# Seven block products for eight in the up projection of an MLP, with the down projection cut into pieces that follow it

## The chip, the cores and the metric

The kernel runs on one core of a Trainium2 chip. The metric is the device time of one execution in microseconds (us). The program is one launch with five instruction streams: TensorE (PE in the profile) multiplies matrices, VectorE (DVE), ScalarE (ACT) and GpSimd (POOL) do elementwise work, SyncE (SP) issues the loads of weights. Streams meet only at semaphores that the code counts by hand. Each stream runs in program order, so an instruction that waits holds up everything behind it on its engine.

## The reference, cut to what matters

Two blocks work on a 1024 x 1024 activation in float32: first an attention layer and a convolution layer, then a recurrent mixer and an MLP. Only the MLP at the end is changed:

```python
h = rms_norm_2(x, norm_mlp[l])
x = x + jnp.square(jax.nn.relu(h @ w_up[l])) @ w_down[l]   # w_up 1024 x 4096, w_down 4096 x 1024
return rms_norm_2(x, norm_final)
```

## The kernel before, in words

**Layout.** Everything stays in SBUF with channels on the 128 partitions and 1024 tokens along the free axis. `X[:, k, :]` is channel tile k (0 to 7) of the residual stream. A matmul takes a weight tile of 128 x 128 and 512 tokens and accumulates into one PSUM bank of 512 float32. PSUM has eight banks; `acc(0)` is banks 0 and 1, `acc(1)` banks 2 and 3, `bank(b)` one of them.

**Split operands.** TensorE works in the rounded type fp32r, so each operand is kept as a high part and the remainder: `Whi`, `Wlo` for weights, `Hh`, `Hl` for the normalised input, `Bh`, `Bl` for other activations. Each product is a triple (`triple`, lines 1500 to 1502): high x high, high x low, low x high.

**A unit.** A unit is one weight slab of 1024 rows x 128 columns: eight tiles, two halves of the tokens, three matmuls, so 48 matmuls (`whole`, `half`). SyncE loads the slab into `Wraw[:, slot]`, ScalarE copies it to `Whi` once TensorE is done with the slab two units before (line 487), GpSimd subtracts to get `Wlo` (line 404), and TensorE waits for that (`claim`). There are two slots, so a slab is prepared while the one before it is multiplied.

**The MLP.** 4 rounds (`for c in range(4)`): eight units of `w_up`, then eight of `w_down` over the 1024 hidden channels just made. ScalarE applies relu (`ut`), VectorE squares it (`sq2`, line 1472), ScalarE copies the square to `Bh`, VectorE subtracts to get `Bl` (line 1475). A down unit is added to `X` by VectorE (line 1479). The last eight down units go by token halves (`by_halves`, called from line 2057, with `projection(3, ...)` on the other engines): units 0 and 1 whole, then six half-token pieces of the first half and six of the second, 24 matmuls each. While these run, the final norm is built up: for each piece n VectorE adds PSUM to `X` (`residual`, line 1260), ScalarE squares (line 506), VectorE adds the square to `sacc` (`add_square`, line 924). After the first token half TensorE sums `sacc` over the channels with a matrix of ones (`square_sum`, line 1544), ScalarE takes the root (line 510), VectorE the reciprocal (line 929) and scales two tiles per piece (line 935). The second token half then ends in the same way, and the results are stored.

**Entry.** The MLP is entered through `opening`: two up units, multiplied half by half as VectorE finishes the normalised input (line 942).

Of the kernel before, what the change touches and what calls it, by code (L numbers as in the profile page):

```python
# [47 lines left out]
def columns_of(params):  # L48
    at, out = 0, {}
    for name, rows in params:  # L50
# [10 lines left out]
          ("rg", 32), ("hg", 40), ("ho", 14), ("mlp", 70)]  # L61
# [49 lines left out]
def build(nc, I, out_dram):  # L111
# [63 lines left out]
    tn = at("tn", T + 12 * KB, [2, 512])  # L175
    Bh = at("Bh", y0, [KT, N], F32R)
# [82 lines left out]
    ut = at("ut", T, [2, N])  # L259
    sq2 = at("sq2", T + 8 * KB, [2, N])  # L260
# [10 lines left out]
    raw_free = sem("raw_free")  # L271
# [10 lines left out]
    DOWN = BASE["mlp"] + 56  # L282
# [17 lines left out]
    w_down = nW["w_down_2"][0].rearrange("(c k p) m -> p c k m", p=P, k=KT)  # L300
# [5 lines left out]
    def sp_program(sp):  # L306
# [23 lines left out]
        for h in range(2):  # L330
            c = slice(h * 512, h * 512 + 512)
            for j in range(4):
                sp.dma_start(X[:, 2 * j:2 * j + 2, c], xk[:, 2 * j:2 * j + 2, c]).then_inc(sem(f"x_loaded{h}{j}"), 16)
# [51 lines left out]
        for c in range(4):  # L385
            for j in range(8):
                unit_at(BASE["mlp"] + 16 * c + j, c * 1024 + j * P, w_up)
            if c < 3:
                for j in range(8):
                    unit_at(BASE["mlp"] + 16 * c + 8 + j, j * P, w_down[:, c, :, :])  # L390
        projection_weights(DOWN, w_down[:, 3, :, :])
# [81 lines left out]

    gate = lambda l: 24 * l + 16
# [3 lines left out]
    def act_program(act):  # L478
# [16 lines left out]
        def projection(i, base, shift):  # L495

            def square(n):
                evacuated(act, 0, 2, base + n)
# [31 lines left out]
        act.wait_ge(sem("eps_set"), 1)  # L530
        act.activation(cs[:, :, 0], P1[:, COL1["c"]:COL1["c"] + 8], ACT.Silu).then_inc(sem("cs_ready"), 1)
        act.activation(cs[:, :, 1], P1[:, COL1["c_ctx"]:COL1["c_ctx"] + 8], ACT.Silu).then_inc(sem("cs_ready"), 1)
        act.wait_ge(sem("lb_shifted"), 1)
        act.activation(small[:, 0:8], small[:, 0:8], ACT.Exp).then_inc(sem("lb_exp"), 1)
        act.wait_ge(sem("lam_abs"), 1)
        act.activation(small[:, 32:40], small[:, 24:32], ACT.Exp, scale=-1.0).then_inc(sem("lam_exp"), 1)
        act.wait_ge(sem("lamsum"), 1)
        act.activation(small[:, 8:10], bank(0, 2), ACT.Exp).then_inc(sem("lamexp"), 1)
        for n in range(2 * KT):
            h, k = n // KT, n % KT  # L540
            act.wait_ge(sem(f"x_loaded{h}{k // 2}"), 16)
# [344 lines left out]
        for c in range(4):  # L886
            for k in range(8):
                u = BASE["mlp"] + 16 * c + k
                if c and k == 0:
                    split_next(0, 2, u)  # L890
                got(act, 0, 2, u)
                split_next(0, 2, u + 1)
                act.wait_ge(sem("ut_free"), c * 8 + (k + 1))
                act.activation(ut[:, k % 2, :], acc(k % 2), ACT.Relu).then_inc(acc_free[k % 2], 1)  # L894
                act.wait_ge(sem("usq_ready"), c * 8 + (k + 1))
                act.activation(Bh[:, k, :], sq2[:, k % 2, :], COPY).then_inc(sem("uh_ready"), 1)
            for k in range(1, 8 if c < 3 else 0):
                split_next(0, 2, BASE["mlp"] + 16 * c + 8 + k)
        projection(3, DOWN, None)


    def dve_program(dve):
        stt, tt, ts = dve.scalar_tensor_tensor, dve.tensor_tensor, dve.tensor_scalar

        def projection(i, base, add_to, gain, shift):

            H, L = ((Bh, Bl), (Bh, Bl), (Hh, Hl), (None, None))[i]

            def residual(n):
                u = base + n  # L910
# [21 lines left out]
            def scaled(h, k):  # L932
# [43 lines left out]
        dve.memset(EPSC, EPS).then_inc(sem("eps_set"), 1)  # L976
# [3 lines left out]
        tt(small[:, 0:8], lbl, lbl, ALU.subtract).then_inc(sem("lb_shifted"), 1)  # L980
# [4 lines left out]
        dve.drain().then_inc(sem("lamprod"), 1)  # L985
# [3 lines left out]
        dve.drain().then_inc(sem("lam_abs"), 1)  # L989
# [57 lines left out]
        dve.wait_ge(sem("lam_exp"), 1)  # L1047
# [24 lines left out]
        dve.wait_ge(sem("lb_exp"), 1)  # L1072
# [12 lines left out]
        dve.wait_ge(sem("lamexp"), 1)  # L1085
# [381 lines left out]
        for c in range(4):  # L1467
            for k in range(8):
                u = BASE["mlp"] + 16 * c + k
                dve.drain()  # L1470
                evacuated(dve, 0, 2, u)
                tt(sq2[:, k % 2, :], ut[:, k % 2, :], ut[:, k % 2, :], ALU.mult).then_inc(sem("usq_ready"), 1)  # L1472
                dve.drain().then_inc(sem("ut_free"), 1)
                dve.wait_ge(sem("uh_ready"), c * 8 + (k + 1))
                tt(Bl[:, k, :], sq2[:, k % 2, :], Bh[:, k, :].bitcast(F32), ALU.subtract).then_inc(sem("ul_ready"), 1)
            for k in range(8 if c < 3 else 0):
                u = BASE["mlp"] + 16 * c + 8 + k
                got(dve, 0, 2, u)
                tt(X[:, k, :], X[:, k, :], acc(k % 2), ALU.add).then_inc(acc_free[k % 2], 1)  # L1479
            dve.drain()  # L1480
        projection(3, DOWN, plain, lambda k: P2[:, COL2["norm_final_2"] + k:COL2["norm_final_2"] + k + 1], None)


    def pe_program(pe):
# [56 lines left out]
        def square_sum(i, h):  # L1541

            pe.wait_ge(sem("sq_added"), 12 * i + 5 * h + 7)
            ins = mm(bank(4 + h), ones, sacc[:, h, :], start=True, stop=(h == 0))
            if h:
                pe.wait_ge(sem("sq_ready"), 14 * i + 14)
                ins = mm(bank(5), ones, sqs[:, 1, :], start=False, stop=True)
# [37 lines left out]
        pe.wait_ge(sem("lamprod"), 1)  # L1585
# [35 lines left out]
        def first_products(k, h):  # L1621
# [3 lines left out]
            for u in range(2):  # L1625
                if k == 0 and h == 0:
                    pe.wait_ge(lo_ready, u + 3)
                    pe.wait_ge(sem("lamexp"), 1)
# [6 lines left out]
        pe.wait_ge(sem("cs_ready"), 2)  # L1635
# [414 lines left out]
        for c in range(4):  # L2050
            b = BASE["mlp"] + 16 * c
            for j in range(0 if c else 2, 8):
                whole(b + j, (Hh, Hl))
            pair(b + 8, (Bh, Bl), lambda h, k: pe.wait_ge(sem("ul_ready"), c * 8 + k + 1))
            for j in range(2, 8 if c < 3 else 0):
                whole(b + 8 + j, (Bh, Bl))
# [57 lines left out]
```

## Time and profile before

| what | value |
|---|---|
| median of 3 runs | 2892.82 us (2890.85 to 2893.32) |
| profiled execution, its own time | 2892.7 us |
| its span in the trace | 2890.9 us |
| TensorE busy over the span | 2820.3 us, 98% |
| VectorE, ScalarE, GpSimd busy | 1432.4, 913.5, 627.4 us |
| mean granted TensorE clock | 0.997 of full |

The span runs from the first to the last recorded instruction; the execution's own time is 1.8 us longer. Times in the rows are microseconds from the span's start. The MLP lies from about 2177 to 2891.

### The profile page before, as it was taken

The page shows a single profiled execution, that of the slowest core. Times are in us where ns is not written, and L with a number is a line of the kernel's source. Part 1 is how long each engine was busy: PE and PEld are TensorE (multiplying, and loading weights), DVE is VectorE, ACT ScalarE, POOL GpSimd, SP SyncE. Part 2 cuts the span into 40 slices and gives each one's busy share as a digit, 9 for nine tenths or more (in the row PEclk, how much of TensorE's full clock was granted, in tenths as well). Part 3 has the DMA queues.
Part 4 walks back from the last instruction along what each step waited for, and adds up shares of the span by engine and source line. Part 5 has one row for each costly group of instructions (what it writes and reads, how often), then busy time and mean ns, then how long its engine had stood idle before and what let it go on. Part 6 is the DMA issues. An engine that isn't in the chain of part 4 may idle for free.

```text
span 2890.9 us, 34606 instructions
## 1 busy us (share of the span) xinstructions
PE 2820.3 (98%) x14290; PEld 2338.5 (81%) x14290; DVE 1432.4 (50%) x1518; ACT 913.5 (32%) x1087; POOL 627.4 (22%) x319
## 2 busy tenths in 40 slices
PE   7999999999999999999999999999999999999997
PEld 4878777887788888788888888888777888888886
DVE  6478128877422226545555665656765213131236
ACT  4332217763211113444442222222333112121122
POOL 0111115104222224222221111111142222212222
PEclk9999999999999999999999999999999999999999
DMA  7211440023111112111111111111031111111113
GB/s 225 73 29 39 150 147 1 1 74 95 51 45 51 47 49 84 55 44 44 51 55 37 37 30 37 37 37 37 23 85 54 47 49 44 52 51 51 44 54 114
DMA packets 276884, 168.52 MB, mean 58 GB/s; under 512 B 5632, under 2 KB 270208, under 8 KB 276352
## 3 DMA queue, kind: packets, MB, share of 16 engines
q1 hardware_dynamic: 275296, 162.88, 19.2%
q10 hardware_dynamic: 1440, 3.51, 0.3%
q8 instruction: 113, 1.85, 0.3%
q14 instruction: 35, 0.29, 0.0%
HBM read 162.17 MB, written 4.19 MB: 58 GB/s over the span
## 4 chain that ended last, share of the span: by engine, by line
PE 60%; issue 27%; POOL 5%; DVE 4%; ACT 2%; DVEq 1%; SPq 0%; DMA 0%; POOLq 0%; ACTq 0%
PE PS L1500 16%; PE PS L1502 16%; PE PS L1501 16%; POOL Wlo L404 5%; PE PS L1948 3%; ACT exp L689 1%; DVE acol L1177 1%; PE PS L1676 1%; PE PS L1597 1%; PE PS L1953 1%; PE PS L1813 1%; PE PS L1982 1%; PE PS L1936 0%; PE PS L1685 0%; PE PS L1984 0%
## 5 line engine op out<-in xcount | busy, mean ns | idle before, releaser
L404 POOL TENSOR_TENSOR Wlo<-Wraw,Whi 128x1024 fp32r<-128x1024 f32 x237 | 564.5, 2382 | 1992.2 <-ACT Whi L487 1992.2
L1500 PE MATMUL PS<-Bh,Whi 128*128 128x512 f32 x2176 | 858.6, 395 | 3.5 <-POOL Wlo L404 1.3
L1502 PE MATMUL PS<-Bh,Wlo 128*128 128x512 f32 x2176 | 848.1, 390 | 0.0
L1501 PE MATMUL PS<-Bl,Whi 128*128 128x512 f32 x2176 | 847.5, 389 | 0.0
L487 ACT ACTIVATE Whi<-Wraw 128x1024 fp32r<-128x1024 f32 x237 | 247.2, 1043 | 767.4 <-PE PS L1502 765.1
L1500 PEld LDWEIGHTS PS<-Bh,Whi 128*128 128x128 f32 x2176 | 409.1, 188 | 93.2 <-DVE Bl L942 4.9
L1502 PEld LDWEIGHTS PS<-Bh,Wlo 128*128 128x128 f32 x2176 | 408.7, 188 | 86.3
L1501 PEld LDWEIGHTS PS<-Bl,Whi 128*128 128x128 f32 x2176 | 409.1, 188 | 82.9 <-issue 1.0
L1500 PE MATMUL PS<-Hh,Whi 128*128 128x512 f32 x1120 | 443.9, 396 | 4.9 <-issue 1.7
L1502 PE MATMUL PS<-Hh,Wlo 128*128 128x512 f32 x1120 | 436.2, 389 | 0.0
L1501 PE MATMUL PS<-Hl,Whi 128*128 128x512 f32 x1056 | 411.2, 389 | 0.0
L1500 PEld LDWEIGHTS PS<-Hh,Whi 128*128 128x128 f32 x1120 | 210.3, 188 | 57.7 <-issue 12.4
L1502 PEld LDWEIGHTS PS<-Hh,Wlo 128*128 128x128 f32 x1120 | 210.2, 188 | 44.4
L1501 PEld LDWEIGHTS PS<-Hl,Whi 128*128 128x128 f32 x1056 | 198.3, 188 | 41.6 <-issue 1.7
L1472 DVE TENSOR_TENSOR sq<-ut 128x1024 f32<-128x1024 f32 x32 | 83.7, 2616 | 197.0 <-ACT ut L894 197.0
L1479 DVE TENSOR_TENSOR X<-X,PS 128x1024 f32<-128x1024 f32 x24 | 29.3, 1221 | 214.3 <-PE PS L1502 214.3
L1336 DVE COPY_PREDICATED hP<-mk,PS 127x512 f32<-127x512 int32 (+6 forms) x56 | 50.1, 894 | 105.4 <-PE PS L1948 105.2
L1948 PEld LDWEIGHTS PS<-hZ 128*127 128x127 f32 (+6 forms) x896 | 93.1, 176 | 8.2 <-issue 3.1
L1948 PE MATMUL PS<-hZ 128*127 128x64 f32 (+6 forms) x896 | 93.7, 257 | 2.3 <-DVE hZ L1350 2.1
L689 ACT ACTIVATE exp<-PS,acol 128x1280 f32<-128x1280 f32 x60 | 79.6, 1327 | 43.9 <-DVE acol L1179 43.6
L924 DVE TENSOR_TENSOR sacc<-sacc,sqs 128x512 f32<-128x512 f32 x44 | 75.5, 1716 | 25.6 <-ACT sqs L506 25.6
L1840 PE MATMUL PS<-vT,probT 128*128 128x128 f32 x640 | 76.8, 275 | 0.4 <-ACT osq L703 0.4
(329 smaller groups left out, 3083.9 us busy)
## 6 DMA issues: line engine op xcount, KB each, us to landing
Wraw<-in_w_in SPq DMA_DIRECT2D x64, 512.0 KB, 4.0
Wraw<-in_w_down SPq DMA_DIRECT2D x38, 512.0 KB, 3.7
adaV<-in_ada_w SPq DMA_DIRECT2D x16, 1024.0 KB, 5.2
Wraw<-in_odd_w_in SPq DMA_DIRECT2D x32, 512.0 KB, 4.1
Wraw<-in_w_up SPq DMA_DIRECT2D x32, 512.0 KB, 4.1
Wraw<-in_even_w_in SPq DMA_DIRECT2D x24, 512.0 KB, 3.8
adaW<-in_ada_w SPq DMA_DIRECT2D x8, 1024.0 KB, 11.3
Wraw<-in_even_w_out SPq DMA_DIRECT2D x14, 512.0 KB, 3.8
```

The source lines that it names most:

```text
L404: pool.tensor_tensor(Wlo[:, slot, 0:tiles, :], Wraw[:, slot, 0:tiles, :], Whi[:, slot, 0:tiles, :].bitcast(F32), ALU.subtract).then_inc(lo ...
L487: act.activation(Whi[:, slot, 0:tiles, :], Wraw[:, slot, 0:tiles, :], COPY).then_inc(hi_ready, 1)
L689: act.activation(weights_of(b, m)[:, :], PS[:, (S0, S1)[m]:(S0, S1)[m] + NK], ACT.Exp, bias=acol[:, b % 3, 5 + m:6 + m], accum_out=acol[:, ...
L924: tt(sacc[:, h, :], sacc[:, h, :], sqs[:, n % 2, :], ALU.add).then_inc(sem("sq_added"), 1)
L1336: dve.copy_predicated(hP[0:r, :].rearrange("p (c b two l) -> p c b two l", c=8, two=2, l=L)[:, :, :, 1, :], mk[lev][0:r, :].rearrange("p ( ...
L1472: tt(sq2[:, k % 2, :], ut[:, k % 2, :], ut[:, k % 2, :], ALU.mult).then_inc(sem("usq_ready"), 1)
L1479: tt(X[:, k, :], X[:, k, :], acc(k % 2), ALU.add).then_inc(acc_free[k % 2], 1)
L1500: mm(out, Whi[:, u % 2, k, :], hi[:, k, c], start=(k == 0), stop=False)
L1501: mm(out, Whi[:, u % 2, k, :], lo[:, k, c], start=False, stop=False)
L1502: return mm(out, Wlo[:, u % 2, k, :], hi[:, k, c], start=False, stop=(k == KT - 1))
L1840: ins = mm(rows_in(b), probT[:, b % 2, t, :], vT[:, t, h * P:(h + 1) * P], start=(t == 0), stop=(t == 9))
L1948: ins = mm(bank(4 + lev % 2, 64, c * 64)[0:P - L].rearrange("p (b l) -> p b l", l=L), z[:, 0:P - L], right, start=True, stop=True)
```

## The change

The first four up units stay as they were, and a down piece over their 512 hidden channels follows at once. The other 28 up units are taken two at a time, 14 pairs. A pair is a 256-column slab of `w_up` times 1024 tokens. It is cut into 2 x 2 blocks (rows of weights 0 to 511 and 512 to 1023 against two output tiles; channels against token halves), and its four output quadrants C11, C12, C22, C21 are made from seven block products (Strassen in Winograd's form) in place of eight. A block product is 4 tiles x 3 matmuls = 12 matmuls of 512 tokens.

- **Token sums.** Four sums of blocks of the normalised input are made once, before the pairs (`difference`, and the plain `tt` beside it), split into high (`token_high`) and low (`token_low`, for the last block VectorE inside pair 0).
- **Weight sums.** Four sums of blocks of weights per pair are made by GpSimd (`first_sums`, `second_sum`, `third_sum`), and each of the seven blocks is split as before, by halves of a slot (`block_high` on ScalarE, `part_low` on GpSimd). A block's high part is written once the product four before it is done.
- **Products.** They share banks: products 3, 4 and 5 are added onto what a bank holds, after ScalarE has copied the earlier value out (`product_out`). VectorE adds the copy and the bank (`quadrant`), squares with relu in one instruction (`squared`), ScalarE makes the high part (`u_high`), VectorE the low (`quadrant_low`).
- **Down pieces.** After each odd pair but the last (2 pairs = 4 hidden tiles) come four down units of 48 matmuls. The first of them uses the four older quadrants first, and asks for the newest low parts in two steps.
- **End.** The last four hidden tiles are multiplied in 14 steps (`last_products`): two of 24 matmuls, then twelve of 12.
- **Memory.** Two more raw slots and a sum buffer are placed in memory gained by `dynamic_dma_scratch_size=1024`; some semaphores are merged.

The diff, cut to its core:

```diff
-          ("rg", 32), ("hg", 40), ("ho", 14), ("mlp", 70)]
+          ("rg", 32), ("hg", 40), ("ho", 14), ("mlp", 4)]
...
+    BUF_OF = {C11: 0, C12: 1, C22: 2, C21: 0}
+    COPIED = {0: (C11, 3), 2: (C22, 1), 3: (C12, 3), 5: (C21, 3)}
+    FINAL = {C11: (1, 0), C12: (4, 1), C22: (5, 3), C21: (6, 2)}
...
 # SyncE
+        def pair_loads(g):
+            n = pair_load(g)
+            for u in range(2):
+                sp.wait_ge(sem("up_lo"), down_event(g // 2 - 1, 2 * (g % 2) + u) + 1)
+                col = (FIRST + 2 * g + u) * P
+                raw_load(n + u, raw_of(n + u), w_up[:, :, col:col + P])
...
 # GpSimd
+        token_low(0)
+        down_low(-1, 0)
+        down_low(-1, 1)
+        token_low(1)
+        token_low(2)
+        down_low(-1, 2)
+        down_low(-1, 3)
+        for g in range(PAIRS):
+            first_sums(g)          # 2 sums, drain
+            second_sum(g)          # low part of block 0, 1 sum, drain
+            third_sum(g)           # low part of block 1, 1 sum, drain
+            other_lows(g)          # low parts of blocks 2 to 6, drain
+            if g % 2 and g < 12:
+                for d in range(4):
+                    down_low(g // 2, d)
...
 # ScalarE
+        def product_out(g, i):
+            q, b = COPIED[i]
+            act.wait_ge(sem("product"), 7 * g + i + 1)
+            if q == C21:
+                act.wait_ge(sem("ul_ready"), 8 + 4 * g + 1)
+            else:
+                act.wait_ge(sem("ul_ready"), 4 + 4 * g + (4 if q == C11 or g == 0 else q + 1))
+            act.activation(cbuf[BUF_OF[q]][:, :], pair_bank(g, b), COPY).then_inc(sem("product_out"), 1)
...
+        first_relu(0)
+        first_u(0)
+        token_high(0)
+        first_relu(1)
+        first_u(1)
+        token_high(1)
+        token_high(2)
+        first_relu(2)
+        down_high(-1, 0)
...
+        for g in range(PAIRS):
+            for i in range(7):
+                p = 7 * g + i
+                if i == 0 and g % 2:
+                    u_high(g - 1, C21)
+                if i in COPIED:
+                    product_out(g, i)
+                if not ends or i < 3:
+                    block_high(p + 4)
+                elif c == RUNS - 1:
+                    last_high(i - 3)
+                elif i in (4, 6):
+                    down_high(c, i // 2 - 2)
+                if i in (2, 5, 6):
+                    u_high(g, {2: C11, 5: C12, 6: C22}[i])
+                if g == 0 and i == 1:
+                    act.wait_ge(sem("down_psum"), SMALL)
+                    token_high(3)
...
 # VectorE
+        for k in range(4):
+            first_half_again(k, k)             # one scalar_tensor_tensor each
+        for k in range(4):
+            first_half_again(12 + k, 4 + k)
+        dve.drain()
+        for k in range(4):
+            difference(k, 8 + k, k)
+        first_squares(0)                       # 2 squares, 2 low parts
+        for k in range(4):
+            tt(Tf[:, 8 + k, :], Tf[:, 4 + k, :], Tf[:, 8 + k, :], ALU.subtract)
+        first_squares(1)
+        for k in range(4):
+            difference(4 + k, 4 + k, k)
+        dve.drain()
+        for k in range(4):
+            difference(12 + k, 12 + k, 4 + k)
+        first_squares(2)
+        first_squares(3)
...
+        for g in range(PAIRS):
+            quadrant(g, C11)
+            quadrant_low(g, C11)
+            if g == 0:
+                ...                            # 4 low parts of the fourth token block
+            quadrant(g, C12)
+            quadrant(g, C22)
+            quadrant_low(g, C12)
+            quadrant(g, C21)
+            quadrant_low(g, C22)
+            quadrant_low(g, C21)
...
 # TensorE
+        PRODUCT_BANK = (3, 0, 1, 3, 1, 3, 2)
+        def product(g, i):
+            p = 7 * g + i
+            out = pair_bank(g, PRODUCT_BANK[i])
+            pe.wait_ge(sem("up_lo"), block_event(p) + 1)
+            if i in (3, 4, 5):
+                pe.wait_ge(sem("product_out"), 4 * g + {3: 1, 4: 2, 5: 3}[i])
+            if g == 0 and i in (2, 3, 5, 6):
+                pe.wait_ge(sem("t_lo"), {2: 4, 3: 8, 5: 12, 6: 16}[i])
+            for k in range(4):
+                hi, lo = token_block(i, k)
+                ins = three(out, ..., k, hi, lo, ...)       # 3 matmuls of 512 tokens
+            ins.then_inc(sem("product"), 1)
...
+        for n in range(2, 14):
+            h = 0 if n < 8 else 1
+            pe.wait_ge(sem("up_lo"), last_event(n) + 1)
+            pe.wait_ge(sem("last_free"), n - 1)
+            last_products(n, h, (0, 1), halves[0])
+            if n == 9:
+                square_sum(3, 0)
+            last_products(n, h, (2, 3), halves[0]).then_inc(sem("last_ready"), 1)
...
-    nc = bacc.Bacc("TRN2", target_bir_lowering=False, num_devices=1)
+    nc = bacc.Bacc("TRN2", target_bir_lowering=False, num_devices=1, dynamic_dma_scratch_size=1024)
```

Four things in words. `down_low(-1, 0)` stands behind `token_low(0)`, which waits for eight `difference` steps. The high part of the fourth up unit is made in `first_relu(1)`, behind `first_u(0)` and `token_high(0)`. `last_free` is raised by VectorE's `residual`; `square_sum(3, 0)` has moved from the middle of piece 8 to the middle of piece 9. `last_high(n + 4)` stands ahead of the square of piece n.

## Rows read from the trace of the kernel before

**Rows 1.** The page, busy time and share of the span of each engine.

```profile
PE 2820.3 (98%) x14290; PEld 2338.5 (81%) x14290; DVE 1432.4 (50%) x1518; ACT 913.5 (32%) x1087; POOL 627.4 (22%) x319
```

**Rows 2.** Windows inside the MLP: bounds, length, each engine's busy time (instructions), granted clock, DMA.

```profile
2400.00:2600.00 200.00, 200.00 (x884) 165.62 (x883) 49.29 (x29) 38.80 (x38) 43.07 (x18) 1.00 0.17 50
```

**Rows 3.** Groups of instructions by form, 2197.9 to 2875.2: count, busy us, mean ns, idle before.

```profile
L1500 PE MATMUL PS<-Bh,Whi 128*128 128x512 f32 x512 | 199.6, 390 | 0.0
```

**Rows 4.** Groups of instructions by form, GpSimd.

```profile
L404 POOL TENSOR_TENSOR Wlo<-Wraw,Whi 128x512 fp32r<-128x512 f32 x8 | 10.3, 1287 | 68.7 <-ACT Whi L487 68.7
```

**Rows 5.** Groups of instructions by form, ScalarE.

```profile
L510 ACT ACTIVATE Rn<-PS,Dv 128x512 f32<-128x512 f32 x8 | 5.5, 687 | 21.3 <-PE PS L1544 13.5 <-PE PS L1547 7.8
...
L487 ACT ACTIVATE Whi<-Wraw 128x512 fp32r<-128x512 f32 x8 | 5.0, 621 | 0.0
```

**Rows 6.** Timeline of the end: start, length, engine, line, operation, idle before.

```profile
2840.15 0.69 DVE L1260 TENSOR_TENSOR X<-X,PS 128x512 f32<-128x512 f32 x1 [1.29 <-PE PS L1502]
2841.82 2.45 DVE L924 TENSOR_TENSOR sacc<-sacc,sqs 128x512 f32<-128x512 f32 x1 [0.98 <-ACT sqs L506]
2846.21 3.35 DVE L929 RECIPROCAL Rn<-Rn 128x512 f32<-128x512 f32 x1 [1.94 <-ACT Rn L510]
2849.64 0.69 DVE L1260 TENSOR_TENSOR X<-X,PS 128x512 f32<-128x512 f32 x1
2851.03 1.35 DVE L924 TENSOR_TENSOR sacc<-sacc,sqs 128x512 f32<-128x512 f32 x1 [0.70 <-ACT sqs L506]
...
2857.74 0.68 DVE L924 TENSOR_TENSOR sacc<-sacc,sqs 128x512 f32<-128x512 f32 x1
...
2870.59 1.41 DVE L935 SCALAR_TENSOR_TENSOR X<-X,P,Rn 128x512 f32<-128x512 f32 x2
...
2875.43 0.69 DVE L1260 TENSOR_TENSOR X<-X,PS 128x512 f32<-128x512 f32 x1 [2.83 <-PE PS L1502]
```

**Rows 7.** The same timeline: TensorE, ScalarE and GpSimd around 2841 to 2846.

```profile
2844.33 1.13 PE L1544 MATMUL PS<-sacc,basic 128*128 128x512 f32 x2 [1.50 <-DVE sacc L924]
...
2845.49 0.69 ACT L510 ACTIVATE Rn<-PS,Dv 128x512 f32<-128x512 f32 x1 [3.70 <-PE PS L1544]
...
2841.35 2.38 POOL L404 TENSOR_TENSOR Wlo<-Wraw,Whi 128x1024 fp32r<-128x1024 f32 x1 [3.04 <-ACT Whi L487]
```

**Rows 8.** Timeline, VectorE and GpSimd together in the attention stage and before the MLP.

```profile
447.50 0.46 POOL L448 TENSOR_TENSOR ql<-qT,qh 128x128 fp32r<-128x128 f32 x1
...
447.51 1.79 DVE L1195 SCALAR_TENSOR_TENSOR exp<-exp,acol,exp 128x1280 f32<-128x1280 f32 x1
...
447.89 2.52 POOL L437 CAST kh<-kT 128x1280 fp32r<-128x1280 f32 x1
...
2157.16 0.69 DVE L1260 TENSOR_TENSOR X<-X,PS 128x512 f32<-128x512 f32 x1
...
2157.25 2.40 POOL L404 TENSOR_TENSOR Wlo<-Wraw,Whi 128x1024 fp32r<-128x1024 f32 x1 [3.03 <-ACT Whi L487]
```

**Rows 9.** Timeline of the MLP's entry: VectorE, ScalarE, GpSimd.

```profile
2191.55 1.63 DVE L942 SCALAR_TENSOR_TENSOR Hl<-tn,Dv,Hh 128x512 fp32r<-128x512 f32 x2
...
2194.32 1.06 ACT L487 ACTIVATE Whi<-Wraw 128x1024 fp32r<-128x1024 f32 x1 [1.92 <-PE PS L1502]
...
2195.46 2.39 POOL L404 TENSOR_TENSOR Wlo<-Wraw,Whi 128x1024 fp32r<-128x1024 f32 x1 [18.80 <-ACT Whi L487]
```

**Rows 10.** Windows shortly before the MLP, columns as in rows 2.

```profile
2072.00:2076.00 4.00, 1.24 (x6) 1.25 (x7) 3.92 (x6) 0.11 (x1) 0.00 (x0) 0.53 0.00 0
2076.00:2080.00 4.00, 4.00 (x14) 3.26 (x13) 3.82 (x5) 1.02 (x1) 0.00 (x0) 0.62 0.00 0
```

**Rows 11.** Timeline of TensorE in the second of these windows.

```profile
2078.23 0.63 PE L1501 MATMUL PS<-Bl,Whi 128*128 128x512 f32 x1
2078.66 0.58 PE L1502 MATMUL PS<-Bh,Wlo 128*128 128x512 f32 x1
```

**Rows 12.** The page, DMA issues: KB each, median us from issue to landing.

```profile
Wraw<-in_w_up SPq DMA_DIRECT2D x32, 512.0 KB, 4.1
```

More of the change, by code:

```diff
@@ new lines, in act_program @@
+        down_high(-1, 2)
+        down_high(-1, 3)
+        for j in range(4):
+            block_high(j)
+        for g in range(PAIRS):
+            c = g // 2
+            ends = g % 2
+            for i in range(7):
[15 more added lines that the diff above has]
+                    token_high(3)
+            if ends:
+                u_high(g, C21)
+                if c < RUNS - 1:
+                    down_high(c, 2)
+                    down_high(c, 3)
+                    for j in range(4):
+                        block_high(14 * (c + 1) + j)
@@ new lines, in u_low, with first_squares @@
+        def u_low(b, tiles, n):
+            dve.wait_ge(sem("uh_ready"), n)
+            tt(tiles[1], cbuf[b][:, :], tiles[0].bitcast(F32), ALU.subtract).then_inc(sem("ul_ready"), 1)
+        def first_squares(u):
+            for h in range(2):
+                n = 2 * u + h
+                dve.wait_ge(sem("relu_out"), n + 1)
+                squared(FIRST_BUF[n], n)
+            for h in range(2):
+                n = 2 * u + h
+                u_low(FIRST_BUF[n], first_u_tiles(u, h), n + 1)
@@ new lines, in quadrant, with quadrant_low @@
+        def quadrant(g, q):
+            i, b = FINAL[q]
+            dve.wait_ge(sem("product"), 7 * g + i + 1)
+            dve.wait_ge(sem("product_out"), 4 * g + {C11: 1, C22: 4, C12: 3, C21: 4}[q])
+            buf = cbuf[BUF_OF[q]]
+            tt(buf[:, :], pair_bank(g, b), buf[:, :], ALU.add).then_inc(sem("quadrant_out"), 1)
+            dve.drain()
+            squared(BUF_OF[q], 8 + 4 * g + q)
+        def quadrant_low(g, q):
+            t, h = tiles_of(g)[q]
+            u_low(BUF_OF[q], (u_tile(Uh, Hh, t, h), u_tile(Ul, Hl, t, h)), 8 + 4 * g + q + 1)
@@ L2049, in pe_program, with three @@
         opening(2, BASE["mlp"], (Hh, Hl))
[L2050 to L2056, printed above, removed]
-        by_halves(3, DOWN, (Bh, Bl))
+        def three(out, place, w, hi, lo, first, last, onto=False):
+            mm(out, place(Whi, w), hi, start=first, stop=False, skip_group_check=onto)
+            mm(out, place(Whi, w), lo, start=False, stop=False, skip_group_check=onto)
+            return mm(out, place(Wlo, w), hi, start=False, stop=last, skip_group_check=onto)
@@ new lines, in pe_program @@
+        PRODUCT_BANK = (3, 0, 1, 3, 1, 3, 2)
[7 more added lines that the diff above has]
+                pe.wait_ge(sem("t_lo"), {2: 4, 3: 8, 5: 12, 6: 16}[i])
+            for k in range(4):
+                hi, lo = token_block(i, k)
+                ins = three(out, lambda W, n: part_of(W, block_place(p))[:, n, :], k, hi, lo, k == 0 and i in (0, 1, 2, 6), k == 3, i in (3, 4, 5))
+            ins.then_inc(sem("product"), 1)
@@ new lines, in pe_program, with last_products @@
+        for d in range(4):
+            down_unit(-1, d)
+        for g in range(PAIRS):
+            pair_banks_free(g)
+            for i in range(7):
+                product(g, i)
+            if g % 2 and g < 12:
+                for d in range(4):
+                    down_unit(g // 2, d)
+        def last_products(n, h, ks, c):
+            for k in ks:
+                ins = three(last_acc(n)[:, c], lambda W, m: part_of(W, last_place(n))[:, m, :], k,
+                            u_tile(Uh, Hh, k, h), u_tile(Ul, Hl, k, h), k == 0, k == 3)
+            return ins
```

406 lines of the change are left out of this document (337 added, 69 removed).

## Prediction

> **What bounds the kernel now.** I read four views in this order. The page's first part first: TensorE is busy 98% of the span, no other engine over 50% [rows 1]. Then the windows of the MLP: 200.00 of 200 us busy, 884 matmuls, clock full [rows 2]. The reader is to see the pace there, 200/884 = 0.2262 us for a matmul of 512 tokens; TensorE is not waiting, it is fully fed. Then the groups by form: the matmuls of the down units have 0.0 us of idle ahead of them [rows 3]. From 2197.9 to 2875.2 TensorE runs 2976 such matmuls; less 1.1 us for the two of ones and 1.5 us of waiting [rows 7], that is 674.7/2976 = 0.2267 us, which I use. Last the timeline, for what the other engines cost when they meet. So removed matmuls are worth their full time, and added work elsewhere is free until it makes TensorE wait.
>
> **What is removed.** Up before: 32 units x 48 = 1536 matmuls. After: 4 x 48 + 14 pairs x 7 products x 12 = 192 + 1176 = 1368. Down before 1536, after 8 x 4 x 48 less the last round, 7 x 192 + 2 x 24 + 12 x 12 = 1344 + 192 = 1536, the same. Removed: 168 matmuls x 0.2267 = **38.1 us**. A product of 12 lasts 2.72 us, a pair 19.04 (21.76 before), a down unit 10.88.
>
> **What is added, and where it hides.** GpSimd, per pair: 4 sums and 7 low parts, 11 instructions over 512 columns. The nearest row is 1.287 us [rows 4]; 14.2 us, under 19.04. ScalarE: 7 high parts and 4 high parts of quadrants at 0.62, 4 copies out of PSUM, of which the nearest row has 0.69 [rows 5]: 9.6 us. VectorE: 4 additions from PSUM at 0.69 [rows 6], 4 squares at 0.7 (1.41 for two) and 4 low parts at 0.68 [rows 6]: 8.3 us. Each fits alone. Cover is what TensorE has queued: a block's low part is ready up to four products (10.9 us) ahead.
>
> **The shared path.** VectorE's addition of two SBUF tiles takes 0.68 us alone [rows 6], but the one that started at 2841.82 took 2.45: GpSimd's subtraction ran 2841.35 to 2843.73 [rows 6, 7], and VectorE ended 0.54 after it. One with an operand in PSUM is not held (0.69 at 2157.16, beside GpSimd's 2157.25 [rows 8]). They take turns: VectorE's 1.79 began at 447.51, GpSimd's next, issued at 447.89, ended 1.11 us after it [rows 8]. The Trainium skill (GPSIMD Engine Reference, Specifications) says the same of the SBUF interfaces, which GpSimd shares with VectorE instructions that have two SBUF inputs; this trace agrees, 2.45 against 0.68. By that rule 8 of VectorE's 12 instructions per pair and all 11 of GpSimd's exclude each other.
>
> Both kinds together take 11 x 1.287 + 8 x 0.54 = 18.5 us of 19.04 in a pair. But down units follow each second pair with four low parts in 43.5 us, so only a lag within two pairs counts. One held VectorE instruction costs up to 1.287 + 0.54 = 1.83. I followed the tightest loop, from the last product of an even pair (time 0) to the odd pair's product 3, wanted at 3 x 2.72 = 8.2: it needs the old C21's low part, then a 0.7 copy. With every instruction held, C22 is squared at -0.1, C12's low part is done at 1.75, C21 is added at 2.5, squared at 4.4, low parts of C22 and C21 at 6.2 and 8.0, the copy at 8.7: late by 0.5. GpSimd's lead runs out before that (its next block must wait for this very copy), so the last two are not held. I take 0, bound 7 x 0.5 = 3.5. GpSimd from product 2 of the even pair (1.3 after it): 8 instructions x 1.287 + 7 turns x 0.54 = 15.4 until the odd pair's third block is ready, wanted at 4 + 2 products = 16.3: 0 again.
>
> **Pair 0.** Here VectorE has four more low parts, of the token block for product 6, behind C11's. From product 2's end: C11's high part 2.3, its low part 4.1, four held at 1.83 = 11.4; product 6 is due at 8.2. Stall between 0 and 3.3, taken **3.0**, since GpSimd has seven instructions in a row there.
>
> **Entry.** VectorE's last low part ends at 2193.2 [rows 9]. Then 8 instructions at 0.67, interrupted by GpSimd's subtraction (2195.46, 2.39 long): 2201.0; 4 differences 2203.6. Only then the first squares, 2205.0. GpSimd's subtraction waits for the one in progress, so the third up unit starts 2198.3, **0.4** later than before. ScalarE does `first_u(0)` (2205.7), `token_high(0)` (2208.1) and only then the fourth unit's high part (1.06, 2209.1); GpSimd its low part (2.39), 2211.6. TensorE is through with the third at 2209.2: wait **2.4**. The down piece's first low part stands behind `token_low(0)`, which needs eight differences. VectorE: low parts 2206.3, 4 subtractions 2208.8, squares held by GpSimd 2213.0, low parts 2214.3, differences 2216.8. Then 4 x 1.287 against 4 differences x 0.54 in turns: 2224.1; `down_low(-1, 0)` 2226.5. The fourth unit ends at 2222.5: wait **3.9**. Both waits have no cover; bounds 1 for the two together (the same chain with no instruction held) and 9.
>
> **End.** Count from the end of piece 7. Before, GpSimd held `add_square(7)`, so TensorE waited 1.5 [rows 7]. Now `square_sum(3, 0)` stands in piece 9, at 4.1. From it to the next `residual` is 1.16 to the root (2844.33 to 2845.49), 0.72 to the reciprocal, 3.43 to `residual(8)` (2849.64) [rows 6, 7]: 9.4. Piece 10 waits for that residual (10.0) and was due at 6.6. After it VectorE sets the pace: `residual` to `add_square` 1.39 (2849.64 to 2851.03), that 0.7, then four times 0.65 + 1.41 + 0.7, about 2.75 with 0.05 between: 13.3, so `residual(13)` at 22.7, plus 0.6 where GpSimd's last low part holds it: 23.3. TensorE alone would have it at 6 x 2.72 + 1.13 = 17.5, so 5.8 is waiting. Before, it came at 2875.43 - 2840.12 = 35.3 [rows 6], against 33.8: 1.5. The same work of VectorE now meets pieces half as long: net **+4.3**. What follows (2875.43 to the end) is the same. Bounds: +3 to +7.
>
> **Loads.** A slab lands 4.1 us after issue [rows 12]; the tightest is wanted more than a pair later. The last steps' half slabs are issued four steps (10.9) ahead: 0. GpSimd's and ScalarE's longer straight-line code, merged semaphores, the smaller descriptor memory: nothing waits on them in the rows, 0.
>
> **Clock.** After some matmul-poor microseconds the granted clock fell to 0.53 and 0.62 of full [rows 10], and 512-token matmuls came 0.43 us apart [rows 11], six in all, the 1.2 GHz level: 6 x 0.20 = 1.2 us. A wait of 1.5 us did not do it [rows 7]. Waits of 3 to 4 us are new here. I take one fall, **1.2**; bounds 0 and four falls, 4.8. The Trainium skill (TensorE: Matmul & The Clock Gate, What's actually happening) calls the slow state the default that activity releases. By that rule each long wait would be followed by a slow stretch.
>
> **Sum.** -38.1 + 0.4 + 2.4 + 3.9 + 3.0 + 4.3 + 1.2 = -22.9. The profiled execution took 2892.7 (span 2890.9, 1.8 around it), 0.1 under the median, so both give the same: 2892.7 - 22.9 = 2869.8, I say **2869.5**, span 2867.7.
>
> **Rivals.**
> A, the waits hide: 1 us at the entry, none in pair 0, the end as above: -38.1 + 4.3 + 1 = 2860. For it: my worst cases hold every instruction. Against: the entry's order is written down.
> B, the shared path sets the pace of pairs: if an instruction's start doesn't overlap the other's turn, 11 x 1.287 + 8 x (0.69 + 0.05 handover) = 20.1 per pair. 14 x (20.1 - 19.04) = 15 more: 2884. For it: 18.5 of 19.04 was already tight. Against: the down units give the lag back.
> C, slower: C21's chain makes product 3 of every odd pair wait. It decides where W plus a clock fall reaches 22.9/7 = 3.3 us, W = 2.1, that is a chain of 10.3 us for my 8.7 at most. At 12 us, 7 x (3.8 + 1.2) = 35: 2905. For it: seven engine changes in a row, each with a handover that I priced at 0.1. Against: 1.6 us beyond the bound. The clock page's rule, with a fall behind each wait, works in this direction.
> D, the gain is not there: 12-matmul products with three waits run at 0.2267 + 0.0082 = 0.235, 2808 x 0.0082 = 23 us lost, no change. Against: 24-matmul pieces show no such loss at their seams.
>
> **Chances.** Forecast 0.62, A 0.16, B 0.13, C 0.05, D 0.04. A measurement of this kernel can't tell changes under 0.2% (5.8 us) from none. Faster 0.91 (forecast, A, B), same 0.04 (D), slower 0.05 (C). The range takes in A below and B above: **2857 to 2888**.
>
> **What would show it.** In the trace after: 168 fewer 512-token matmuls at 0.227; one wait of TensorE of about 2.4 before the fourth up unit and one of 3.9 before the first down unit; one in pair 0 before product 6; none in later pairs; about 3.4 before piece 10 of the end; VectorE's squares in the pairs longer than 0.7 wherever GpSimd runs. I would be wrong if GpSimd's sums cost much more than 1.287, if TensorE waits in every pair on a copy or a low part, or if falls of the clock follow the waits and last.

## The result, and the profile after

The changed kernel takes 2868.65 us (2868.06 to 2869.2), against 2893.07 for the kernel before beside it: ratio 0.9918, 95% interval 0.9903 to 0.9933. It is faster by 24.4 us, 0.84%. On a second chip the ratio was 0.9919 (0.9906 to 0.9933). The forecast was 2869.5, a gain of 23. The profiled execution's own time is 2868.1, its span 2866.3, 24.6 less than before.

The page, busy time of each engine:

```profile
PE 2787.2 (97%) x14122; PEld 2309.0 (81%) x14122; DVE 1549.4 (54%) x1698; ACT 955.1 (33%) x1241; POOL 785.3 (27%) x461
```

Against [rows 1] TensorE has 14290 - 14122 = 168 matmuls fewer, as counted. VectorE has 117 us more, ScalarE 42, GpSimd 158. The windows say whether that costs anything:

```profile
2400.00:2600.00 200.00, 200.00 (x884) 165.58 (x884) 78.96 (x72) 46.73 (x74) 93.37 (x61) 1.00 0.16 48
...
2300.00:2800.00 500.00, 500.00 (x2208) 414.01 (x2207) 212.76 (x198) 131.50 (x213) 245.79 (x161) 1.00 0.17 52
```

Through 500 us of pairs and down units TensorE doesn't stop once, at the same 884 matmuls in 200 us as in [rows 2]. VectorE and GpSimd do far more than before and are hidden. So the price must lie at the ends. The waits of TensorE from 2135 on (who waited for whom: us in total, times, longest):

```profile
PE PS L2434 <- DVE X L1575: 3.6, 1, 3.6
PE PS L2434 <- POOL Wlo L645: 3.0, 1, 3.0
PE PS L1882 <- POOL Wlo L530: 2.0, 2, 1.3
PE PS L2434 <- DVE Tl L1852: 1.8, 1, 1.8
```

In this order they are the end (piece 10 waits for `residual(8)`), the first down unit (`down_low(-1, 0)`), the third and fourth up unit (0.7 and 1.3), and pair 0's product 6. Before, TensorE waited 1.5 at the end, for the sum [rows 7], and 0.3 ahead of the third up unit:

```profile
PE PS L1500 <- POOL Wlo L404: 0.3, 1, 0.3
```

This view counts idle time only. Lost time is the distance of two starts less the pace of 0.227: 1.4 us for the fourth up unit, 3.2 for the first down unit, 2.0 for product 6. The timeline shows what followed the 3.0, and the wait at the end:

```profile
2224.36 0.50 PE L2434 MATMUL PS<-Uh,Whi 128*128 128x512 f32 x1 [3.00 <-POOL Wlo L645]
2224.70 0.57 PE L2435 MATMUL PS<-Ul,Whi 128*128 128x512 f32 x1
2225.07 0.63 PE L2436 MATMUL PS<-Uh,Wlo 128*128 128x512 f32 x1
2225.49 0.63 PE L2434 MATMUL PS<-Uh,Whi 128*128 128x512 f32 x1
...
2837.08 0.77 PE L2434 MATMUL PS<-Uh,Whi 128*128 128x512 f32 x1 [3.63 <-DVE X L1575]
```

From the third on, starts are 0.43 apart, as in [rows 11], up to 2228.0; added up over nine distances, 1.6 us more is lost. I call a matmul slow when the next one starts 0.4 us or more after it: there are seven here. The granted clock of that window is 0.59, and 0.50 after the wait of 3.6 at the end, where 12 matmuls are slow:

```profile
2224.00:2228.00 4.00, 3.63 (x9) 2.88 (x10) 3.90 (x6) 3.11 (x6) 0.31 (x1) 0.59 0.47 131
...
2837.00:2841.00 4.00, 3.92 (x9) 3.14 (x10) 3.28 (x5) 1.75 (x3) 1.28 (x1) 0.50 0.00 0
```

Now the engines that caused this. Timeline of the entry and of pair 0, VectorE, ScalarE, GpSimd:

```profile
2192.71 7.51 DVE L1785 SCALAR_TENSOR_TENSOR Tf<-X,P,Rn 128x512 f32<-128x512 f32 x8
...
2212.60 9.52 DVE L1788 TENSOR_TENSOR Tf<-Tf 128x512 f32<-128x512 f32 x8
...
2206.65 1.04 ACT L681 ACTIVATE Whi<-Wraw 128x1024 fp32r<-128x1024 f32 x1
...
2215.16 6.40 POOL L611 TENSOR_TENSOR Tl<-Tf,Th 128x512 fp32r<-128x512 f32 x4 [5.03 <-ACT Th L1092]
2221.53 2.78 POOL L645 TENSOR_TENSOR Wlo<-Wraw,Whi 128x1024 fp32r<-128x1024 f32 x1
...
2280.95 6.85 DVE L1852 TENSOR_TENSOR Tl<-Tf,Th 128x512 fp32r<-128x512 f32 x4
2287.72 0.68 DVE L1812 TENSOR_TENSOR cbuf<-PS,cbuf 128x512 f32<-128x512 f32 x1
2288.49 1.00 DVE L1791 SCALAR_TENSOR_TENSOR cbuf<-cbuf 128x512 f32<-128x512 f32 x1
...
2291.13 1.78 DVE L1795 TENSOR_TENSOR Ul<-cbuf,Uh 128x512 fp32r<-128x512 f32 x1
```

Eight differences, 5 us when alone, take 9.5 while GpSimd's four token parts take 6.4 for 5.1: both lose by taking turns. GpSimd reaches the down piece's low part (2.78 for 2.40) only at 2221.5. In pair 0 four instructions of 0.68 take 6.85, 1.71 each; I had used 1.83. The last three rows show the sign that I had named: the addition from PSUM keeps its 0.68, the square beside it takes 1.00 for 0.7, the low part 1.78 for 0.68.

The end, VectorE's timeline, to be read beside [rows 6]:

```profile
2827.16 0.69 DVE L1575 TENSOR_TENSOR X<-X,PS 128x512 f32<-128x512 f32 x1
...
2832.82 3.35 DVE L1242 RECIPROCAL Rn_end<-Rn_end 128x512 f32<-128x512 f32 x1 [3.05 <-ACT Rn_end L709]
2836.25 0.69 DVE L1575 TENSOR_TENSOR X<-X,PS 128x512 f32<-128x512 f32 x1
...
2842.58 0.69 DVE L1575 TENSOR_TENSOR X<-X,PS 128x512 f32<-128x512 f32 x1 [1.29 <-PE PS L2436]
...
2850.84 0.69 DVE L1575 TENSOR_TENSOR X<-X,PS 128x512 f32<-128x512 f32 x1
```

From the end of piece 7 (2827.1) to `residual(8)` is 9.1 us, to `residual(13)` 23.7. The 1.29 of idle time at 2842.58 is VectorE waiting for TensorE, slowed by its clock.

### The profile page after: what moved, and what is told of

The parts are those of the page before. It is cut to its first block, busy times and chain, and to the rows that moved or that the text cites. A ratio compares the mean times of both kernels' runs of the same rounds, so it can differ in the third digit from the quotient of the medians.

```text
span 2866.3 us, 34875 instructions
## 1 busy us (share of the span) xinstructions
PE 2787.2 (97%) x14122; PEld 2309.0 (81%) x14122; DVE 1549.4 (54%) x1698; ACT 955.1 (33%) x1241; POOL 785.3 (27%) x461
## 3 DMA queue, kind: packets, MB, share of 16 engines
q8 instruction: 112, 1.84, 0.3%
## 4 chain that ended last, share of the span: by engine, by line
PE 60%; issue 25%; DVE 5%; POOL 5%; ACT 3%; DVEq 1%; DMA 0%; SPq 0%; ACTq 0%; POOLq 0%
PE PS L1882 9%; PE PS L1884 9%; PE PS L1883 9%; PE PS L2434 7%; PE PS L2436 7%; PE PS L2435 7%; POOL Wlo L530 5%; PE PS L2331 3%; ACT exp L892 1%; DVE acol L1492 1%; PE PS L2059 1%; PE PS L2336 1%; PE PS L1980 1%; PE PS L2196 1%; PE PS L2365 1%
## 5 line engine op out<-in xcount | busy, mean ns | idle before, releaser
L530 POOL TENSOR_TENSOR Wlo<-Wraw,Whi 128x1024 fp32r<-128x1024 f32 (+1 forms) x171 | 406.8, 2379 | 1491.8 <-ACT Whi L681 1491.7
L1882 PE MATMUL PS<-Bh,Whi 128*128 128x512 f32 x1664 | 659.0, 396 | 3.6 <-POOL Wlo L530 1.3
L1884 PE MATMUL PS<-Bh,Wlo 128*128 128x512 f32 x1664 | 648.8, 390 | 0.0
L1883 PE MATMUL PS<-Bl,Whi 128*128 128x512 f32 x1664 | 648.1, 389 | 0.0
L1882 PEld LDWEIGHTS PS<-Bh,Whi 128*128 128x128 f32 x1664 | 312.9, 188 | 73.3 <-DVE Bl L1257 5.2
L1884 PEld LDWEIGHTS PS<-Bh,Wlo 128*128 128x128 f32 x1664 | 312.4, 188 | 66.3
L681 ACT ACTIVATE Whi<-Wraw 128x1024 fp32r<-128x1024 f32 (+1 forms) x171 | 177.2, 1036 | 329.6 <-PE PS L1884 327.2
L604 POOL TENSOR_TENSOR Wlo<-Wraw,Whi 128x512 fp32r<-128x512 f32 x84 | 113.7, 1361 | 118.7 <-ACT Whi L1135 114.4
L645 POOL TENSOR_TENSOR Wlo<-Wraw,Whi 128x1024 fp32r<-128x1024 f32 x28 | 69.2, 2472 | 150.3 <-ACT Whi L1147 150.3
L2434 PE MATMUL PS<-Uh,Whi 128*128 128x512 f32 x256 | 101.1, 395 | 6.7 <-DVE X L1575 3.6
```

Of the source, the lines that this page charges most:

```text
L530: pool.tensor_tensor(Wlo[:, slot, 0:tiles, :], Wraw[:, slot, 0:tiles, :], Whi[:, slot, 0:tiles, :].bitcast(F32), ALU.subtract).then_inc(lo ...
L604: pool.tensor_tensor(part_of(Wlo, block_place(p)), raw, part_of(Whi, block_place(p)).bitcast(F32), sub).then_inc(sem("up_lo"), 1)
L645: pool.tensor_tensor(slot_of(Wlo, down_place(c, d)), raw_of(down_load(c, d)), slot_of(Whi, down_place(c, d)).bitcast(F32), sub).then_inc(s ...
L681: act.activation(Whi[:, slot, 0:tiles, :], Wraw[:, slot, 0:tiles, :], COPY).then_inc(hi_ready, 1)
L1882: mm(out, Whi[:, u % 2, k, :], hi[:, k, c], start=(k == 0), stop=False)
L1883: mm(out, Whi[:, u % 2, k, :], lo[:, k, c], start=False, stop=False)
```

## The experiments

Where runs are compared by their traces, the stretch is from the first matmul of the third up unit (2197.74 in the changed kernel, 2197.4 to 2199.2 in others, since the part before the MLP varies) to the span's end: 668.6 us in the changed kernel, 693.0 in the kernel before. Two kernels were traced twice, and their stretches agree to 0.1 us. The kernels with more sums, with the filled wait and with one order changed were executed once each.

**Eight products instead of seven.** Is the gain the matmuls, with all other costs left in place?

```diff
-            for k in range(4):
+            for k in list(range(4)) * (2 if i == 6 else 1):
                 hi, lo = token_block(i, k)
```

> The changed kernel with product 6 of each pair made twice (the same result again, 12 redundant matmuls per pair), so eight products as in an ordinary multiplication, while all else of the change stays. Theory (TensorE sets the pace of the pairs, the gain is the 168 matmuls): 168 x 0.2267 = 38.1 us more than the changed kernel, 2868.7 + 38.1 = 2906.8, which is 13.7 over the kernel before; that 13.7 is the price of the entry, pair 0 and the end. Rival (GpSimd and VectorE, which take turns, set the pace of the odd pairs, and the gain comes from elsewhere): the odd pairs absorb their share, 19 us or less are added, about 2888.

Measured: 2907.29 us, ratio to the kernel before 1.0051 (1.0034 to 1.0067); on the stretch 706.7 us, 38.1 more than 668.6. TensorE's waits are those of the changed kernel to 0.1 us. The 168 matmuls are worth all of their time, and with them put back the change is a loss of 14 us. The rival falls.

**One more sum on GpSimd per pair, and three.** How near are the pairs to the shared path?

```diff
+            for again in range(1):        # 3 in the second kernel
+                pool.tensor_tensor(S3[:, :, :], top[:, 0:4, :], bot[:, 0:4, :], sub)
+                pool.drain()
             pool.tensor_tensor(S3[:, :, :], top[:, 0:4, :], bot[:, 0:4, :], sub).then_inc(sem("s_ready"), 1)
```

> The changed kernel with one more sum on GpSimd per pair (the first weight sum made twice, same result). Theory (GpSimd has 2.8 us to spare in an odd pair: the low part of its third block ends at 2375.2, wanted at 2378.0): the extra 1.29 + 0.16, with a turn of VectorE at most 2.0, leaves TensorE without a wait, span 2866.3 within 1. Rival (the shared path is already the limit): 7 odd pairs x 1.5 to 2.0 = 10 to 14 us more, span 2877 to 2880.

> The same with three more sums per pair. Theory (2.8 us to spare per odd pair, then every us of GpSimd is a us of TensorE): 3 x 1.45 = 4.4, with turns of VectorE up to 6.0, so 1.6 to 3.2 of waiting in each of 7 odd pairs, 11 to 22 us more, span 2877 to 2888, and in the trace waits of TensorE on GpSimd's low parts in odd pairs only. Rival (nothing in the pairs hangs on GpSimd): span unchanged.

Measured: with one, span 2867.9, 1.6 more than 2866.3, but 1.5 of that lies before the third up unit; the stretch is 668.7, 0.1 more, and TensorE is busy 500 of 500 us from 2300 to 2800. With three, span 2883.6, stretch 685.5, 17.0 more. Waits of TensorE in that kernel:

```profile
PE PS L2437 <- POOL Wlo L604: 10.8, 20, 1.1
PE PS L2437 <- DVE X L1578: 3.6, 1, 3.6
```

The 20 waits lie in the seven odd pairs (g = 1, 3 and so on, the second of each two), none in an even one, three per pair but for one that has two. Three sums add 3 x (1.29 + 0.16 for the drain) = 4.4 us to a pair; 10.8 / 7 = 1.5 of idle time, or 17.0 / 7 = 2.4 of the stretch, is lost per odd pair. So an odd pair had 2 to 3 us of room, and beyond it GpSimd sets the pace. Rival B of the prediction was one and a half to two more sums away, and in the odd pairs only.

**Filling the wait.** Is the slow stretch a consequence of the wait?

```diff
             for h in range(2):
                 for k in range(KT):
                     last = triple(u, k, ...)
+            if u == UP + 3:
+                for k in range(4):
+                    last = three(bank(7), lambda W, n: W[:, u % 2, n, :], k, Hh[:, k, 512:1024], Hl[:, k, 512:1024], k == 0, k == 3)
             last.then_inc(acc_ready, 1)
```

> The changed kernel with 12 redundant matmuls of 512 tokens after the fourth up unit, into a bank that the first down unit starts afresh, so that TensorE works through 2.7 of the 3.2 us for which it waits there. The low part it waits for does not depend on them. Theory (the slow stretch of nine matmuls at 2224 to 2228 follows from the wait): the first down unit starts at the same 2224.4, at 0.227 us per matmul instead of 0.43, and 1.6 us are saved, span 2864.7. Rival (the slow stretch has another cause): matmuls from 2224.4 are 0.43 us apart as before, span 2866.3.

Measured: span 2863.4, stretch 666.0, 2.5 less, with 12 matmuls more. The wait is 0.3, and the window after it has the clock at 1.00 with 17 matmuls where there were 9:

```profile
2224.00:2228.00 4.00, 3.94 (x17) 3.28 (x18) 3.66 (x6) 3.41 (x6) 0.18 (x2) 1.00 0.46 131
```

The slow stretch came from the wait, and 1.6 of the 2.5 are its time. The other 1.0 has nothing to do with the edit as far as the trace shows: in this run the slow stretch at the end was shorter, 7 slow matmuls instead of 12 after the same wait of 3.6, for a reason that I did not find.

**The fourth unit's weights first.**

```diff
         first_relu(0)
+        first_relu(1)
         first_u(0)
         token_high(0)
-        first_relu(1)
         first_u(1)
```

> ScalarE's first_relu(1), which holds the fourth up unit's high part, stands ahead of first_u(0) and token_high(0). Theory (the 1.4 us wait before the fourth unit is this queue order): the high part is made by about 2198.4, the fourth unit starts when the third ends, at 2208.7, 0 wait. The wait before the first down unit stays tied to eight differences on VectorE, which now come about 2 us earlier because GpSimd's subtraction no longer cuts into the second squares: TensorE reaches it 1.4 earlier, wait 2.5 to 4. Span 2864 to 2866.3. Rival (VectorE, not the order, sets the fourth unit): the wait stays 1.4.

Measured: span 2868.0, stretch 669.1, 0.5 more. The wait before the fourth unit is gone, as the theory said, but the one before the down piece grew from 3.0 to 4.4, and the slow stretch behind it by three matmuls. GpSimd and VectorE in this kernel:

```profile
2199.45 2.89 POOL L530 TENSOR_TENSOR Wlo<-Wraw,Whi 128x1024 fp32r<-128x1024 f32 x1 [0.57 <-ACT Whi L681]
...
2194.57 8.99 DVE L1785 SCALAR_TENSOR_TENSOR Tf<-X,P,Rn 128x512 f32<-128x512 f32 x7
```

GpSimd's subtraction no longer cuts into the second squares, but now into the eight instructions (L1785) with which VectorE's entry begins. Differences and down low part end where they did: 26.4 us after the third unit's start, for 26.6. I had expected 2 us less, and was wrong there: the entry is one chain, and shortening one link of it alone moves the wait.

**The down piece's low part ahead of the tokens'.**

```diff
-        token_low(0)
         down_low(-1, 0)
+        token_low(0)
         down_low(-1, 1)
```

> GpSimd's down_low(-1, 0) stands ahead of token_low(0). Theory (the 3.2 us wait is token_low(0) in front of it): GpSimd waits only for ScalarE's high part, which ends at 2219.8, so the low part ends at 2222.2 or, held by VectorE, 2222.8; the wait falls from 3.2 to 1.0 to 1.6 us and the clock does not fall there, since waits of 2.0 and less were not followed by a slow stretch: 1.6 to 2.2 + 1.6 saved, span 2862.5 to 2863.3. Rival (ScalarE's order holds it back as much): wait still over 2.5.

Measured: span 2864.9, stretch 666.1, 2.5 less where 3.2 to 3.8 were expected. The wait fell to 0.9 without a slow stretch, which is worth 2.1 + 1.6, and a new wait of 0.3 stands inside the first down unit. But now a slow stretch of 7 matmuls, 1.6 us, stands behind pair 0's wait, which is as long as before (1.84 of idle). The stretch would have shown still less of a gain, had the slow stretch at the end not been short in this run too (8 slow matmuls, 1.0 us less). Windows of this kernel, and of the changed one at the same place:

```profile
2288.00:2292.00 4.00, 4.00 (x13) 3.16 (x12) 3.82 (x5) 1.39 (x3) 3.06 (x3) 0.66 0.00 0
```

```profile
2288.00:2292.00 4.00, 4.00 (x18) 3.29 (x19) 3.81 (x5) 1.59 (x3) 3.84 (x3) 1.00 0.01 4
```

So "waits of 2.0 and less are not followed by a slow stretch" is false: the same wait had one here and none there.

**The last token block before pair 0.**

```diff
-                if g == 0 and i == 1:
-                    act.wait_ge(sem("down_psum"), SMALL)
-                    token_high(3)
...
+        act.wait_ge(sem("down_psum"), SMALL)
+        token_high(3)
         for g in range(PAIRS):
...
-            quadrant(g, C11)
-            quadrant_low(g, C11)
             if g == 0:
                 ...
+            quadrant(g, C11)
+            quadrant_low(g, C11)
```

> The four low parts of the last token block, and ScalarE's four high parts, stand ahead of pair 0's first quadrant instead of behind it. Theory (the 2.0 us wait before product 6 of pair 0 is VectorE being held by GpSimd in four instructions in a row): they end 8 us or less into pair 0, product 6 does not wait, 2.0 saved, span 2864.3. Rival (the wait comes from the quadrants before, not from these four): a wait of 1 us or more remains in pair 0, at another product or the same.

Measured: span 2863.4, stretch 665.4, 3.1 less. No wait is left in pair 0 at all, and none elsewhere came for it; 2.0 are this wait. The rest is again a shorter slow stretch at the end (7 slow matmuls, 1.0 us less).

**The end in another order.**

```diff
-                if n == 8:
+                if n == 8 and i < 3:
                     invert(0)
                 residual(n)
+                if n == 8 and i == 3:
+                    invert(0)
-                if 9 <= n < 13:
+                if 9 <= n < (13 if i < 3 else 11):
...
+            if i == 3:
+                for k in range(4, 8):
+                    scaled(0, k)
             invert(1)
...
             h = 0 if n < 8 else 1
+            if n == 9:
+                square_sum(3, 0)
...
-            if n == 9:
-                square_sum(3, 0)
```

> At the end: residual(8) ahead of the reciprocal, the sum over the channels one half piece earlier, and the scaling of four tiles of the first token half put into the gap after residual(13). Theory (VectorE's order makes TensorE wait 3.8 us before piece 10, and its load of work delays residual(13)): no wait before piece 10, no fall of the clock there, residual(13) at 17.8 us after the end of piece 7 instead of 23.7, 5 to 6 us saved, span 2860.5 to 2861.5. Rival (VectorE's total work after the reciprocal sets the end whatever the order): residual(13) still later than 21, at most 3 saved.

Measured: span 2862.7, stretch 664.0, 4.6 less. Waits at the end 0.9 and 0.4 in place of 3.6, no slow stretch, and `residual(13)` 19.1 us after the end of piece 7 (2828.19 to 2847.25), for 23.7. I had said 17.8: the reciprocal began at 2832.74, 4.6 after piece 7, but the addition of a square behind it was held by GpSimd (1.23 for 0.69) and stood ahead of `residual(9)`:

```profile
2832.74 3.35 DVE L1242 RECIPROCAL Rn_end<-Rn_end 128x512 f32<-128x512 f32 x1 [1.15 <-ACT Rn_end L709]
2836.17 1.23 DVE L1237 TENSOR_TENSOR sacc_end<-sacc_end,sqs_end 128x512 f32<-128x512 f32 x1
2837.49 0.69 DVE L1580 TENSOR_TENSOR X<-X,PS 128x512 f32<-128x512 f32 x1
```

**All orders together.** The last three edits, and ScalarE's entry as: `first_relu(0)`, `first_relu(1)`, `first_u(0)`, `token_high(0)`, `first_u(1)`, `token_high(1)`, `first_relu(2)`, `down_high(-1, 0)`, `token_high(2)`.

> The three orders that saved time alone (down_low(-1, 0) first, the last token block ahead of pair 0, the end's order) together with ScalarE's entry reordered throughout: first_relu(1) right behind first_relu(0), and first_relu(2) and down_high(-1, 0) ahead of token_high(2). Theory (each wait is a place in a hand-written queue, and the entry's two waits go only together): no wait before the fourth unit or the first down unit (its low part ready by about 2218.6, wanted at 2219.6), none over 0.8 in pair 0, 0.9 left at the end, no fall of the clock: 668.6 - 1.4 - 3.2 - 1.6 - 2.0 - 4.6 = 655.8 us from the third unit's start to the end, time 2855 to 2857, 0.4% under the changed kernel and 1.25% under the kernel before. Rival (waits only move to the next queue, as the first one did when the fourth unit's weights were made earlier alone): 661 or more, time 2861 or more.

> The changed kernel itself on the same chip, for a direct comparison: 2868.7 within 0.1%.

Measured on one chip: 2859.32 us, ratio to the kernel before 0.9885 (0.987 to 0.99), and 2868.91 for the changed kernel. Stretch 658.6, 10.0 less, where the theory had 12.8. The two entry waits went together, as it said (0.7 is left of the second), but a new one of 1.7 stands in the first down unit, before the tile that the fourth up unit made. So 2.8 of 12.8 us, about a fifth, behaved as the rival says. The median, 2859.32, is over the 2855 to 2857 that I expected. VectorE before that tile:

```profile
2218.45 3.49 DVE L1795 SCALAR_TENSOR_TENSOR cbuf<-cbuf 128x512 f32<-128x512 f32 x2
2221.86 3.49 DVE L1799 TENSOR_TENSOR Th<-cbuf,Th 128x512 fp32r<-128x512 f32 x2
2225.27 3.48 DVE L1795 SCALAR_TENSOR_TENSOR cbuf<-cbuf 128x512 f32<-128x512 f32 x2
```

Pairs of instructions that take 1.29 alone take 3.49 here, all against `token_low(0)` and the two down low parts.

**The tokens' low parts spread.**

```diff
         down_low(-1, 0)
-        token_low(0)
         down_low(-1, 1)
+        token_low(0)
         token_low(1)
-        token_low(2)
         down_low(-1, 2)
+        token_low(2)
```

> The kernel with all orders, and GpSimd's entry spread further: down_low(-1, 0), down_low(-1, 1), token_low(0), token_low(1), down_low(-1, 2), token_low(2), down_low(-1, 3). Theory (of the 2.3 us still lost in the entry, 1.7 are VectorE's squares and low parts of the third and fourth unit, held in turns by token_low(0)): VectorE's eight instructions there run at 0.65 instead of about 1.75, the wait before the fourth unit's tile is gone, the one before the first down unit (0.7, ScalarE and GpSimd behind eight differences) stays; 656.9 us from the third unit's start to the end instead of 658.6, time about 2857.5. Rival (these low parts wait for ScalarE's order, not for GpSimd): no change, 2859.3.

> The kernel with all orders on the same chip, for a direct comparison: 2859.3 within 0.1%.

Measured on one chip: 2856.67 us, ratio to the kernel before 0.988 (0.9863 to 0.9896), beside 2859.17 for all orders alone. Stretch 656.2 where 656.9 was expected, and the wait of 1.7 is gone; waits left 0.7, 0.7, 0.8, 0.4 and 0.3. This version beats both kernels, the changed one by 12.4 us on the stretch.

## Why the prediction was right

| step | forecast, us | measured, us |
|---|---|---|
| 168 matmuls x 0.2267 | -38.1 | -38.1 (eighth product put back) |
| third unit's start | +0.4 | +0.4 (wait 0.7 for 0.3, ahead of the stretch) |
| wait before the fourth unit | +2.4 | +1.4 |
| wait before the first down unit | +3.9 | +3.2 |
| pair 0, product 6 | +3.0 | +2.0 |
| later pairs | 0 | 0 |
| end, net of 1.5 before | +4.3 | +4.7 |
| clock | +1.2 | +1.6 at the entry, and 1.0 to 1.5 of the end's 4.7 |
| seams | 0 | +0.7 |
| sum | -22.9 | -24.5 without the second row; the stretch itself says -24.4 |

The measured end is (23.7 - 17.5) - 1.5. Seams are small losses that belong to no wait. From the third unit's start to the end of the last matmul of 512 tokens are 653.1 us. Less 2808 x 0.2267, the two matmuls of ones (1.1), the lost time of the four waits (1.4, 3.2, 2.0, 3.8) and of the two slow stretches (1.6, 2.5), 0.9 is left, against 0.2 before. That the sum came within 1.5 us is in part luck: single terms were off by up to 1.0 us, the waits mostly too long, the end, the clock and the seams too short.

**The bound and the main term** were right, and the eighth product shows it. **The shared path** worked as read from the rows: instructions with two SBUF inputs held, those with PSUM not, turns one by one. Its bound of no wait in the pairs was right with little to spare; three more sums per pair broke it, in the odd pairs that I had named. **Pair 0** was mis-sized by 1.0: turns cost 1.71 for my 1.83, C11's own low part 1.36, and the chain began earlier, since ScalarE's 512-column copies follow each other 0.52 apart where I had taken 0.62. The experiment that moved the four instructions removed the wait. **The entry** had the right waits at the right places, 1.7 too long in sum: GpSimd's subtraction was done when VectorE had lost 2.1 us, not 2.4, and ScalarE's copies again took 0.52. **The end** was right in its first half: piece 10 waited for `residual(8)`, 9.1 us after piece 7 for my 9.4. That the whole came within 0.4 us is luck: I had VectorE set the pace from there to `residual(13)`, but it stood still for 1.29 and 0.20 us while TensorE's slow matmuls held it up, a time that I had not counted here; without it VectorE would have been about 1.1 us earlier than forecast. In the three runs with the shorter slow stretch `residual(13)` came 22.7 us after piece 7, a net of 3.7. **The clock** was right in kind: two falls, where I had taken one, 1.6 us and, inside the end's figure, 1.0 to 1.5. The one in the entry was shown to follow from its wait. Not every wait is followed by a fall: those of 1.3 and 1.8 us in the changed kernel were not. **The loads**: TensorE's waits name none.

A was nearer than B: every wait was shorter than forecast but the third unit's, which was as forecast, and the end's. C and D were never near: no pair waits, and the pace is 884 in 200 us with 12-matmul products too.

Left open: why the slow stretch at the end has 12 or 13 slow matmuls in six traces and 7 or 8 in three, with the same wait of 3.6 ahead of it, and why pair 0's wait of 1.8 was followed by one in a single trace of nine.

## What to carry to other kernels

When one engine is busy all the time, count its instructions first: fewer of them is the gain, and work added elsewhere is free until a queue is late. Then walk each place where the pipeline starts, changes or ends, since there the cover is thin; here steady pairs cost nothing and 14 us were lost at the entry, the first pair and the end, 12 of them only through the order of hand-written queues. Move orders together: an order that removes one wait alone may hand it on. And where a gain of 1 us matters, look where in the trace it lies: three runs here gained 1.0 at a place that their edit did not touch.

## What the runs showed of the hardware beyond that

- GpSimd and VectorE in turns slow each other to 1.71 us per VectorE instruction of 512 columns with two SBUF inputs, 2.5 times its 0.68, and eight of them to 9.5 us for 5.0.
- The same wait of TensorE of 1.8 us of idle was followed by full clock in one kernel and by seven matmuls at 0.43 us (granted clock 0.66) in another; waits of 3.0 and 3.6 in the changed kernel were followed by 7 and 12 such matmuls. Twelve redundant matmuls in the wait of 3.0 took no more time than the wait, and the 1.6 us of the slow stretch behind it were saved.
